# Joining pieces of attention work inside the weight stream of a hybrid decoder layer on one Trainium2 core

## The reference, cut to what matters

```python
xn = rms_norm(x, g_mix)
z = xn @ w_in                       # [q | k | v | forget logits | lru x-branch | lru gate-branch]
att = forgetting_attention(q, k_all, v_all, logf_all, n_past)    # 8 heads of 128
xc = causal_conv(xl, conv_buf, w_conv, b_conv)                   # width 4, depthwise
r = sigmoid(xc @ wa + ba); i = sigmoid(xc @ wx + bx)             # 8 blocks of 128
hs = scan(h = a * h + b, a = exp(-8 r softplus(-lam)), b = sqrt(1 - a^2) * i * xc)
lru = gelu(gl) * hs
x = x + concat(rms_norm(att, g_att_out), rms_norm(lru, g_lru_out)) @ w_out
x = x + relu(rms_norm(x, g_ffn) @ w_up)^2 @ w_down
```

## Time and profile before

| | |
|---|---|
| median of 3 runs | 2286.39 us (2285.51 to 2286.99) |
| the profiled execution | 2287.92 us; its span 2286.3 us |
| busy, share of the span | PE 98%, PEld 96%, DVE 70%, ACT 38%, POOL 7% |
| one step of the loop (step 6) | 65.1 us: PE 65.1, DVE 60.5, ACT 28.2 us busy |

### The profile page before, as it was taken

How to read it: one execution, slowest core, us unless ns; L and a number is a source line. 1 busy time by engine, 2 the same in 40 slices (tenths; PEclk the granted TensorE clock), 3 DMA queues, 4 the chain that set the end, 5 groups by cost and what they waited for, 6 DMA issues and landing times.

```text
span 2286.3 us, 50021 instructions
## 1 busy us (share of the span) xinstructions
PE 2245.4 (98%) x19889; PEld 2197.9 (96%) x19889; DVE 1605.0 (70%) x2043; ACT 858.7 (38%) x1201; POOL 154.1 (7%) x194
## 2 busy tenths in 40 slices
PE   7999999999999999999999999999999999999997
PEld 6999999999988999999999999999999999999997
DVE  7349999999984697767576566566566566566563
ACT  5224434343454333343243243243243243243245
POOL 0001111111113031000000000000000000000002
PEclk8999999999999999999999999999999999999998
DMA  6358999999965242333333433433433433433422
GB/s 236 100 161 259 342 336 345 325 323 327 336 238 199 95 148 81 93 114 104 116 111 100 120 110 93 127 110 89 131 110 86 134 107 86 137 101 92 138 91 95
DMA packets 386972, 368.47 MB, mean 161 GB/s; under 512 B 12259, under 2 KB 350596, under 8 KB 385844
## 3 DMA queue, kind: packets, MB, share of 16 engines
q1 hardware_dynamic: 359828, 295.38, 42.2%
q0 software_dynamic: 18608, 67.64, 8.1%
q10 hardware_dynamic: 8448, 4.20, 0.6%
HBM read 354.22 MB, written 12.94 MB: 161 GB/s over the span
## 4 chain that ended last, share of the span: by engine, by line
PE 93%; DVE 3%; ACT 2%; DMA 1%; SPq 1%; issue 0%; DVEq 0%; ACTq 0%
PE PS L1897 40%; PE PS L1901 20%; PE PS L2343 9%; PE PS L2342 9%; PE PS L2341 9%; PE PS L2058 2%; PE PS L2085 1%; PE PS L2106 1%; DVE WL L1214 1%; PE PS L2248 1%; ACT WH L744 0%; PE PS L2096 0%; DMA VR<-in_cache_v 0%; SPq L439 0%; DMA RAW<-in_w_in 0%
## 5 line engine op out<-in xcount | busy, mean ns | idle before, releaser
L1094 ACT ACTIVATE WH<-RAW 128x1024 fp32r<-128x1024 f32 x293 | 304.9, 1057 | 680.8 <-PE PS L1901 521.4
L1648 DVE TENSOR_TENSOR WL<-RAW,WH 128x1024 fp32r<-128x1024 f32 x293 | 358.1, 1222 | 134.4 <-ACT WH L1094 132.8
L1897 PE MATMUL PS<-XH,WH 128*128 128x260 f32 x1952 | 405.2, 289 | 12.4 <-DVE XL L1279 7.2
L1897 PE MATMUL PS<-HH,WH 128*128 128x260 f32 x2048 | 412.5, 282 | 1.4 <-DVE HL L1653 0.7
L1901 PE MATMUL PS<-HH,WL 128*128 128x260 f32 x2048 | 411.6, 282 | 0.0
L1897 PE MATMUL PS<-HL,WH 128*128 128x260 f32 x2048 | 410.9, 282 | 0.0
L1901 PE MATMUL PS<-XH,WL 128*128 128x260 f32 x1952 | 394.1, 283 | 0.0
L1897 PE MATMUL PS<-XL,WH 128*128 128x260 f32 x1952 | 393.8, 283 | 0.0
L1751 DVE TENSOR_TENSOR A<-A,PS 128x520 f32<-128x520 f32 x256 | 177.3, 695 | 264.5 <-PE PS L1901 264.2
L1897 PEld LDWEIGHTS PS<-XH,WH 128*128 128x128 f32 x1952 | 301.9, 189 | 23.2 <-issue 12.2
L1897 PEld LDWEIGHTS PS<-HH,WH 128*128 128x128 f32 x2048 | 314.6, 188 | 2.1 <-issue 1.1
(11 more groups left out here) (335 smaller groups left out, 3082.8 us busy)
## 6 DMA issues: line engine op xcount, KB each, us to landing
KR<-in_cache_k POOLq DMA_DIRECT2D x128, 512.0 KB, 6.1
VR<-in_cache_v SPq DMA_DIRECT2D x128, 512.0 KB, 5.9
RAW<-in_w_up SPq DMA_DIRECT2D x128, 512.0 KB, 4.2
RAW<-in_w_down SPq DMA_DIRECT2D x128, 512.0 KB, 4.4
RAW<-in_w_in SPq DMA_DIRECT2D x82, 512.0 KB, 8.0
RAW<-in_w_out SPq DMA_DIRECT2D x32, 512.0 KB, 5.3
TMP<-in_w_up SPq DMA_DIRECT2D x30, 512.0 KB, 6.0
xT_spill<-A SPq DMA_DIRECT2D x1, 4160.0 KB, 16.4
```

Of the source, the lines that this page charges most:

```text
L1094: nc.scalar.activation(RING_H[SLOT[i]], RB[b], ACT.Copy).then_inc(f_hi, 1)
L1648: V.tensor_tensor(RING_L[SLOT[i]], RB[op_block(i)], RING_H[SLOT[i]].bitcast(F32), ALU.subtract).then_inc(f_lo, 1)
L1897: mm(dsts[c], wh(k), x[:, k, c * HT:(c + 1) * HT], start=first and n == 0 and x is xh, stop=False)
```

## The change

On TensorE three pieces leave places of their own. The transposes of the probabilities go from unit 2, place 15, to place 21, behind the pages of values that stand there (`places` puts values first). The product of probabilities and values goes from unit 2, place 27, to unit 3, place 7, ahead of the transposes of k and v. The gate products go from behind unit 3 into it, to place 21, behind the pages of values. They keep their waits.

On ScalarE the high part of unit 3 is made ahead of the three copies of the transposed probabilities, where it stood behind them and behind unit 1's drain, and the attention result is copied behind unit 2's drain and the high part of the next unit 0, where it stood ahead of both. On VectorE the scores of pages 12 and 13 go from ahead of `conv` to behind the low part of the next unit 0, in the steps from 1 on; step 0 had them there already. No instruction is added or taken away.

```diff
@@ ScalarE, step()
                 if prev:
                     softmax(i - 1)
+                if head:
+                    split_hi(U_L + 3, 2 * i)
                 if prev:
                     transposed(i - 1)
                 if head:
                     rows_out(tile_wait(U_L + 1, 2 * i), vT, VS, i)
-                    split_hi(U_L + 3, 2 * i)
-                if prev:
-                    attended(i - 1)
                 if head:
                     slot = tile_wait(U_L + 2, 2 * i)
...
                     split_hi(U_L + 4, 2 * i)
+                    if prev:
+                        attended(i - 1)
@@ VectorE, step()
                 if head:
-                    if prev:
-                        score(i, range(12, 14))
                     conv(i)
                     if final:
                         head_lo(NH)
                         head_lo(NH + 1)
                     split_lo(U_L + 4, 2 * i)
-                    if not prev:
-                        score(i, range(12, 14))
+                    score(i, range(12, 14))
@@ TensorE, step()
-                if head:
+                def gate_sums():
 
                     pe.wait_ge(gw_full, 32 * (i + 1))
                     pe.wait_ge(conv_done, i + 1)
...
+                extra = {}
+                if head:
+                    extra[3, 21] = gate_sums
...
-                    extra[3, 7] = rows
+                    extra[3, 7] = (lambda: (attend(i - 1), rows())) if prev else rows
                 if prev:
                     extra[0, 15] = lambda: max_rows(i)
                     extra[0, 21] = lambda: max_all(i)
                     extra[1, 5] = head_scores
-                    extra[2, 15] = lambda: transpose_probs(i - 1)
-                    extra[2, 27] = lambda: attend(i - 1)
+                    extra[2, 21] = lambda: transpose_probs(i - 1)
```

More of the change, by code:

```diff
@@ L2202, in rows @@
                     ins.then_inc(vtr_ps, 1)
+                def gate_sums():
+                    pe.wait_ge(gw_full, 32 * (i + 1))
+                    pe.wait_ge(conv_done, i + 1)
+                    if prev:
+                        pe.wait_ge(att_ready, i)
+                    pe.wait_ge(ktok_ready, i + 1)
+                    pe.wait_ge(vtok_ready, i + 1)
+                    for g in range(2):
+                        mm(PS[:, 4 + g, :], GW[:, g, :], XC[:, 0:SEQ], start=True, stop=True)
+                    for g in range(2):
+                        ins = mm(PS[:, 6, g * NB:(g + 1) * NB], GW[:, g, :], XC[:, SEQ:T], start=True, stop=True)
+                    ins.then_inc(gates_ps, 1)
                 extra = {}
                 if head:
+                    extra[3, 21] = gate_sums
                     if not prev:
```

## The result

The changed kernel takes 2295.74 us in the median of 6 runs (2293.78 to 2296.58), the kernel before 2287.08 in the median of the 6 runs beside it (2285.51 to 2287.91). The ratio is 1.0035, with a 95% interval of 1.0023 to 1.0047: slower by 8.7 us. The forecast was 2293.6, or 7.2 more, with a range of 2290.8 to 2297.0.

What follows compares the result with a forecast made beforehand. TensorE, busy throughout a whole loop step, was taken as the bound. Steps 2 to 7 cost 3.1, step 1 2.2 and the chain behind step 7 1.95: 7.2 us more, giving 2293.6 us, range 2290.8 to 2297.

Steps and rivals of the forecast that it cites:

- The moment at which the low part is ready: VectorE ends the fourth unit's low part 36.14 us behind TensorE's resumption after the maximum's broadcast; unit 3 can't start earlier.
- The wait: At unit 3, steps 2 to 7: TensorE arrives at 35.50, before VectorE's weights, losing 0.80 us a step including restart.
- The joins: Three TensorE pieces set beside others in units 2 and 3 save their interruption ends: 0.28 us a step, steps 1 to 7.
- The peg: In the loop, the exponential ends 6.6 us behind the step's start, hidden before VectorE's broadcast maximum with 0.3 to spare.
- Step 1: Later sigmoids delay VectorE's product by 0.8 and the fourth unit's low part; TensorE waits 2.42 at unit 3: +2.2 us.
- The tail: Behind step 7, the first sigmoid comes later and nothing in the chain to the last block's recurrence absorbs it: +1.95 us.
- No wait: Rival at unit 3: VectorE's low part comes in time; 2286.4 us, or 2284.4 if the chain is covered; chance 0.07.
- Swallowed in the tail or in step 1: Rival: step 7's chain and step 1's shift are partly covered, 1.0 and 0.8 us gone: 2291.8 us; chance 0.10.
- Keys that land late: Rival: VectorE waits for key pages ahead of the low part in six steps, up to 5.2 us, 2298.8; chance 0.12.
- The table switch that costs double: Rival: the load behind Gelu holds ScalarE twice 1.28 us, in loop and behind step 7: about 2301 us; chance 0.02.

Runs made afterwards that it cites:

- the second: The unaltered changed kernel measured again beside the kernel before: 2297.62 us in 5 runs, ratio 1.0045.
- the pieces apart: Changed kernel with its three joined pieces separated again by one or two tiles of plain stream, each in its new unit: 2297.37 us, ratio 1.0041.
- the gates first: Changed kernel with the fourth unit's low part ahead of scores of pages 8 and 9, and ScalarE's sigmoids, tanh and exponential ahead of Gelu: 2286.08 us, ratio 0.9994.
- the gates alone: Kernel before with only the gate products moved to unit 3, place 21, and scores of pages 12 and 13 later: 2289.54 us, ratio 1.0010.

## Why the prediction was right, step by step

**The moment at which the low part is ready**, 36.14 behind the resumption, was read right: 572.97 less 536.85 is 36.12. The 1.6 us of margin in the earlier trace rows was spent by moving 2.08 us of work past it.

**The wait** was forecast at 0.80 with its restart and is 0.72. TensorE came at 35.56 instead of 35.50, since the transposes behind the values took 1.07 and not 1.01.

**The joins** are the step that failed, as a term: 0.28 a step was forecast, 0.04 was measured. The forecast took the passage from values straight to transposes at nothing, between bounds of nothing and 0.10, and the passages to the rows' transposes and to the gates it didn't price at all. They are 0.06, 0.07 and 0.10. The reason given, that the values take 1.86 whatever follows, looked at the wrong row: the passage shows in the piece behind. So a step lost 0.72 - 0.04 = 0.68, measured 0.66 to 0.69 (0.57 in step 3, which took 65.25 before), and not 0.52. Over six steps that is 0.8 to 1.0 us over the sum.

**The peg**: the exponential in the loop ended at 6.6 behind the step's start as forecast, and VectorE's wait for the broadcast maximum shrank from 0.88 to 0.23, against 0.3 forecast. It was hidden, but only just.

**Step 1** was forecast at +2.2 and gave +2.64, 0.24 of the excess the joins again. The other 0.2 is a matter of where one counts from: the forecast counted from the step's start, and from there step 1 gave +2.31, since TensorE came to the mark 0.33 earlier and then waited that much longer. Putting the gates back took 1.67 of the 2.64 away. The 1.5 that the lower clock added in another execution had no term.

**The tail** was forecast at 1.95 and measured alone at 2.02. The first sigmoid came 2.12 behind the end of unit 3, against 2.14. TensorE's wait grew by 1.75 and the next ones shrank by 1.26, while VectorE's chain behind the sigmoid moved as a whole: from the split for XL (starts at 666.86 before, 672.41 after) to the maximum M (starts at 675.45 and 681.00) it takes 8.59 us in both traces, without a wait. So the sum of TensorE's waits would have misled here.

**The rivals.** No wait: fell, by seven waits. Swallowed in the tail or in step 1: fell, by 2.02 and 2.64. Keys that land late: true in single steps (0.41 in step 7; 0.68 in step 3 of another execution), not in six. The table switch that costs double: fell. The load behind Gelu stands at 658.61 and the sigmoid starts at 659.90, 1.29 later, where the Trainium skill ("ScalarE: Activation LUTs", What ACT_TABLE_LOAD costs) has 2.66 with the drain. The trace disagrees with it in this place too.

**The median** lay 8.7 above the one before in the first comparison and 10.4 in the second, and the forecast was 7.2. The joins' 0.24 a step, 1.7 in seven steps, less the 0.08 by which the waits of steps 2 to 7 were overpriced, accounts for 1.2 of the 1.5 to the first, and TensorE's longer waits for values behind the last mark (1.8 instead of 1.5) for 0.3. For the second, the profile shows the lower clock behind step 1's wait (1.5) and a late page (0.7). How many executions have them is open, since only one of each set is profiled. The forecast had no term for either, and the second median, 2297.6, lies above its range, which ends at 2297.0. That the first lies within it is in part luck.

## What to carry to other kernels

When an interruption is moved past the point at which two engines meet, take the other engine's moment of readiness from the last point that holds both, and compare it with the new arrival: a stream that never waits can be 1.6 us from waiting. A join of two unlike pieces saves an end and buys a passage, so price the passage before counting the end. And where a wait can't be avoided, look first whether the engine that is waited for does anything ahead of it that isn't due yet; here two pages of scores, exchanged with the low part, gave back 7 of 9 us.

## What the hardware showed

TensorE's granted clock behind a single wait was not the same from one execution to the next. Between step 1's mark and 760 us, it fell to the lower level behind the waits of 3.8 us in all five profiles that had one. Behind the twelve of 1.97 to 2.67 us it fell in five: 1.97, 1.98, 2.04, 2.06 and 2.67 fell, and 1.98, 2.03 (four times), 2.04 and 2.44 didn't. In the kernel with the pieces apart it fell once more, behind two waits for values of 1.55 and 0.68 that stood 1.3 us apart; waits as long as 1.79 and 0.67, in the kernel with the gates first, had none. Each time TensorE stayed at the lower level for 3.4 us, but for two of the waits of 3.8 (the gates alone, the pieces apart), behind which it was 6.8. It cost 1.5 us in step 1, where TensorE is the bound, 0.8 behind the wait for Gelu's output, and nothing that shows where VectorE's chain was the bound: behind the wait of 3.8 (79.91 and 79.96 from step 7's mark to the last one, with 3.4 and 6.8 us of it) and behind the one of 2.04 (77.92, and 77.90 where the clock stayed).

The three passages between pieces of unlike kind that the change makes cost 0.06 to 0.10 us each, with no row of their own: the cost lies in the start-to-start time of the piece behind.
